# Entry of a two-layer decoder kernel: shift products inside the slab steps of the third pair, and no filler matmuls

## The reference

```python
def modulate(h, shift, scale):
    return h * (1 + scale[:, None, :]) + shift[:, None, :]

mod = c_act @ ada_w[l] + ada_b[l]
sh1, sc1, g1, sh2, sc2, g2, sh3, sc3, g3 = jnp.split(mod, N_MOD, axis=-1)
h = modulate(rms_norm(x, ffn1_norm[l]), sh1, sc1)
x = x + 0.5 * g1[:, None, :] * swiglu(h, ffn1_w_in[l], ffn1_w_out[l])
...
g, u = jnp.split(h @ w_in, 2, axis=-1)
return (jax.nn.silu(g) * u) @ w_out
```

## Time and profile before

| | us |
|---|---|
| runs | 2551.80, 2551.59, 2549.71; median 2551.59 |
| profiled execution, its own time | 2553.98 |
| its span, first to last instruction | 2552.1 |
| PE busy | 2525.7 (99%) |
| DVE busy | 1688.9 (66%) |
| ACT busy | 966.1 (38%) |
| mean granted clock | 0.995 |

### The profile page before, as it was taken

How to read it: one execution, slowest core, us unless ns; L and a number is a source line. 1 busy time by engine, 2 the same in 40 slices (tenths; PEclk the granted TensorE clock), 3 DMA queues, 4 the chain that set the end, 5 groups by cost and what they waited for, 6 DMA issues and landing times.

```text
span 2552.1 us, 34962 instructions
## 1 busy us (share of the span) xinstructions
PE 2525.7 (99%) x11604; PEld 2060.6 (81%) x11604; DVE 1688.9 (66%) x2533; ACT 966.1 (38%) x1628; POOL 108.4 (4%) x187
## 2 busy tenths in 40 slices
PE   8999999999999999999999999999999999999998
PEld 6888888788788878888878888877878888788887
DVE  7655678798988575544365557779999866644432
ACT  3322323555544343332242222255554443423223
POOL 3000010000000000000000001100000000000000
PEclk9899999999999999999999999999999999999999
DMA  8455575322223434543335556722323333333332
GB/s 272 143 157 164 162 230 153 89 80 82 86 85 89 127 88 132 163 132 93 99 89 161 160 164 190 230 79 79 90 82 86 87 95 94 91 97 92 96 97 87
DMA packets 467654, 310.99 MB, mean 122 GB/s; under 512 B 10891, under 2 KB 445181, under 8 KB 467576
## 3 DMA queue, kind: packets, MB, share of 16 engines
q1 hardware_dynamic: 444544, 234.91, 31.5%
q0 software_dynamic: 20352, 70.13, 8.5%
q10 hardware_dynamic: 2696, 5.13, 0.7%
HBM read 305.41 MB, written 5.05 MB: 122 GB/s over the span
## 4 chain that ended last, share of the span: by engine, by line
PE 89%; DVE 5%; ACT 2%; DMA 2%; issue 1%; SPq 0%; ACTq 0%; DVEq 0%
PE bank L1482 27%; PE bank L1484 27%; PE bank L1483 27%; PE bank L1756 2%; DMA w_raw<-in_ffn_w_in 2%; PE bank L1734 1%; DVE rstd L809 1%; DVE w_lo L785 1%; PE bank L1504 1%; DVE scaled L820 1%; PE bank L1726 1%; DVE h_lo L829 1%; PE bank L1505 1%; PE bank L1509 1%; ACT w_hi L435 1%
## 5 line engine op out<-in xcount | busy, mean ns | idle before, releaser
L785 DVE TENSOR_TENSOR w_lo<-w_raw,w_hi 128x1024 fp32r<-128x1024 f32 (+1 forms) x428 | 515.1, 1203 | 539.4 <-ACT w_hi L435 538.8
L1482 PE MATMUL bank<-h_hi,w_hi 128*128 128x512 f32 x2096 | 833.3, 398 | 2.8 <-DVE scaled L1131 2.7
L1484 PE MATMUL bank<-h_hi,w_lo 128*128 128x512 f32 x2096 | 817.5, 390 | 0.0
L1483 PE MATMUL bank<-h_lo,w_hi 128*128 128x512 f32 x2096 | 816.3, 389 | 0.0
L435 ACT ACTIVATE w_hi<-w_raw 128x1024 fp32r<-128x1024 f32 (+1 forms) x428 | 445.3, 1040 | 845.8 <-PE bank L1484 795.1
L1482 PEld LDWEIGHTS bank<-h_hi,w_hi 128*128 128x128 f32 x2096 | 393.6, 188 | 88.2 <-issue 6.4
L1484 PEld LDWEIGHTS bank<-h_hi,w_lo 128*128 128x128 f32 x2096 | 393.4, 188 | 84.4
L1483 PEld LDWEIGHTS bank<-h_lo,w_hi 128*128 128x128 f32 x2096 | 394.1, 188 | 77.5 <-issue 0.5
L1247 DVE SCALAR_TENSOR_TENSOR conv_part<-glu,conv_taps,conv_part 128x512 f32<-128x512 f32 x464 | 320.0, 746 | 0.0
L1482 PE MATMUL bank<-s_hi,w_hi 128*128 128x512 f32 x704 | 275.5, 391 | 0.0
L1484 PE MATMUL bank<-s_hi,w_lo 128*128 128x512 f32 x704 | 274.0, 389 | 0.0
(11 more groups left out here) (262 smaller groups left out, 2711.3 us busy)
## 6 DMA issues: line engine op xcount, KB each, us to landing
w_raw<-in_ffn_w_in SPq DMA_DIRECT2D x176, 512.0 KB, 3.9
ada_raw<-in_ada_w POOLq DMA_DIRECT2D x128, 512.0 KB, 4.9
w_raw<-in_w_mix_in SPq DMA_DIRECT2D x112, 512.0 KB, 3.8
w_raw<-in_ffn_w_out SPq DMA_DIRECT2D x64, 512.0 KB, 3.9
w_raw<-in_ffn_w_out SPq DMA_DIRECT2D x32, 384.0 KB, 3.4
ada_first<-in_ada_w SPq DMA_DIRECT2D x16, 512.0 KB, 8.3
w_raw<-in_w_attn_branch SPq DMA_DIRECT2D x16, 512.0 KB, 3.9
w_raw<-in_w_conv_branch SPq DMA_DIRECT2D x16, 512.0 KB, 3.9
```

The lines of the kernel that those rows point to most:

```text
L785: dve.tensor_tensor(wlo[slot][:, 0:n, :], raw[slot][:, 0:n, :], whi[slot][:, 0:n, :].bitcast(F32), ALU.subtract).then_inc(w_lo[slot], 1)
L1482: pe.matmul(acc, wh, hi[:, k0 + k, :], start=first and k == 0, stop=False)
L1483: pe.matmul(acc, wh, lo[:, k0 + k, :], start=False, stop=False)
L1484: mm = pe.matmul(acc, wl, hi[:, k0 + k, :], start=False, stop=last and k == n - 1)
```

## The change

- `third_pair` takes the place of `two_slabs` for pair 2. Slot 1 runs one step behind slot 0, and each of the 16 slab steps has four of the 64 shift-product matmuls between its three large ones: two behind the first, two behind the second.
- `first_sum(1)` moves from behind pair 1 into it (before k=10); the norm's mean moves from k=5 to k=4.
- DVE reads pair 0's bank 0 (`read_plain(0)`) before it reads the shift half's sum, and bank 1 behind `scaled(1)`. The order in `norm_units` becomes w_lo_third(0), low(0), scaled(1), read_plain(1), scaled(2), low(1), w_lo_third(1).
- x's back halves of blocks 0 and 1 are copied by ACT, those of blocks 2 and 3 by DVE.
- The tap transposes come behind the x transposes, in banks TP, and ACT copies them behind the last `plain_hi`. The tap rows lie elsewhere in SBUF.
- All `keep_busy` calls, the tile of ones and its memset are gone.

```diff
@@ ACT @@
-        act.wait_ge(sem("tapsp_ready"), DEPTH)
-        for l in range(DEPTH):
-            act.activation(CW2[...], G[l][:, 0:HEADS * CK], ACT.Copy).then_inc(sem("cw_ready"), 1)
         act.wait_ge(sem("consts"), 3)
         for t in range(QB):
             act.wait_ge(sem("xp_ready"), 2 * t + 1)
             act.activation(X[:, 0:4, t * P:(t + 1) * P], S[0][:, :]..., ACT.Copy).then_inc(sem("x_front"), 1)
+            if t < 2:
+                act.wait_ge(sem("xp_ready"), 2 * t + 2)
+                act.activation(X[:, 4:KT, t * P:(t + 1) * P], (S[1], AUX)[t][:, :]..., ACT.Copy)\
+                    .then_inc(sem("x_back_act"), 1)
...
             plain_hi(0, j)
+        act.wait_ge(sem("tapsp_ready"), DEPTH)
+        for l in range(DEPTH):
+            act.activation(CW2[...], TP[l][:, 0:HEADS * CK], ACT.Copy).then_inc(sem("cw_ready"), 1)
@@ DVE @@
+        def read_plain(t):
+            dve.wait_ge(sem("plain_done"), t + 1)
+            dve.tensor_tensor((F[1], SQ)[t][:, :], G[t][:, :], RSTD[:, :], ALU.mult).then_inc(acc_read[t], 2)
...
             if first:
                 w_lo_third(0)
                 low(0)
-                read_bank(0)
+                scaled(1)
+                read_plain(1)
                 scaled(2)
+                low(1)
                 w_lo_third(1)
-                low(1)
-                read_bank(1)
                 scaled(3)
                 low(2)
...
-        for t in range(QB):
+        for t in (2, 3):
             x_back(t)
...
         for j in range(2, KT):
+            if j == KT // 2:
+                dve.wait_ge(sem("tapsp_ready"), DEPTH)
             plain_lo(0, j)
...
         first_parts(0, 1)
         norm_begin(0, 0)
+        read_plain(0)
         dve.wait_ge(sem("mod_summed"), 1)
@@ PE @@
+        def third_pair(banks, weights, products):
+            for k in range(KT + 1):
+                for slot, n in ((1, k - 1), (0, k)):
+                    if not 0 <= n < KT:
+                        continue
+                    if n == 0:
+                        pe.wait_ge(w_hi[slot], 3)
+                        pe.wait_ge(w_lo[slot], 3)
+                        pe.wait_ge(acc_read[slot], 2)
+                    if slot == 0:
+                        pe.wait_ge(sem("unit_lo"), n + 1)
+                    wh, wl, acc = weights[0][slot][:, n, :], weights[1][slot][:, n, :], banks[slot][:, :]
+                    pe.matmul(acc, wh, HHI[:, n, :], start=n == 0, stop=False)
+                    for part in range(2):
+                        i = 2 * (2 * k - slot) + part
+                        out, pair_weights = products[i // KT]
+                        shift_product(i // KT % 2, i % KT, out, pair_weights)
+                        if part == 0:
+                            pe.matmul(acc, wh, HLO[:, n, :], start=False, stop=False)
+                    mm = pe.matmul(acc, wl, HHI[:, n, :], start=False, stop=n == KT - 1)
+                    if n == KT - 1:
+                        mm.then_inc(w_used[slot], 1)
...
             plain_slabs(0, G, (whi, wlo))
-            plain_slabs(1, TP, nexts, {5: lambda: norm_mean(0, 0)})
-            keep_busy(6, S[0])
             pe.wait_ge(sem("scale0_ready"), 1)
-            first_sum(1).then_inc(sem("mod_summed"), 1)
-            keep_busy(6, S[0])
+            plain_slabs(1, TP, nexts, {4: lambda: norm_mean(0, 0),
+                                       10: lambda: first_sum(1).then_inc(sem("mod_summed"), 1)})
             pe.wait_ge(sem("shift_parts"), 2)
-            keep_busy(6, S[0])
             pe.wait_ge(sem("aux_read"), 1)
-            two_slabs(2, 2, lambda j: pe.wait_ge(sem("unit_lo"), j + 1), weights=thirds,
-                      at={1: lambda: shift_product(0, S[0], (whi, wlo)), 2: lambda: shift_product(1, S[1], (whi, wlo)),
-                          3: lambda: shift_product(0, O, nexts), 4: lambda: shift_product(1, AUX, nexts)})
+            third_pair(G, thirds, ((S[0], (whi, wlo)), (S[1], (whi, wlo)), (O, nexts), (AUX, nexts)))
...
         for n in range(2 * QB):
             t, half = n // 2, n % 2
-            if n == 4:
+            if n == 6:
                 pe.wait_ge(sem("pt_ready"), 1)
                 pe.wait_ge(sem("selg"), 1)
                 first_sum(0).then_inc(sem("scale0_summed"), 1)
             if t and not half:
-                pe.wait_ge(sem("cw_ready"), DEPTH)
-                keep_busy(2, G[1])
                 pe.wait_ge(sem("x_front"), t)
...
         pe.wait_ge(sem("pt_ready"), 1 + DEPTH)
-        keep_busy(8, G[0])
+        pe.wait_ge(sem("taps_in"), 16 * 2 * DEPTH)
+        for l in range(DEPTH):
+            for h in range(HEADS):
+                mm = pe.transpose(TP[l][...], CWR[0:CK, l, h * P:(h + 1) * P], ident[0:CK, 0:CK])
+            mm.then_inc(sem("tapsp_ready"), 1)
...
-        keep_busy(6, S[0])
         pe.wait_ge(sem("sq_ready"), DEPTH * 3 * KT)
```

More of the change, by code:

```diff
@@ L251, in build @@
     BR = at("bias_row", [P, TOK + P], F32, s0 + 12448)
-    CWR = at("tap_rows", [P, DEPTH, D], F32, h0)
+    CWR = at("tap_rows", [P, DEPTH, D], F32, h0 + 24 * KB)
     YO = at("y_rows", [P, QB, D], F32, h0)
@@ L362, in _ @@
         pool.memset(minus_half[:, :], -0.5).then_inc(sem("minus_half"), 1)
-        pool.memset(busy[:, :].bitcast(F32), 1.0).then_inc(sem("busy_ready"), 1)
         pool.wait_ge(sem("ident0"), 1)
@@ L518, in _ @@
                 .then_inc(sem("x_front"), 1)
+            if t < 2:
+                act.wait_ge(sem("xp_ready"), 2 * t + 2)
+                act.activation(X[:, 4:KT, t * P:(t + 1) * P], (S[1], AUX)[t][:, :].rearrange("p (j t) -> p j t", t=P), ACT.Copy)\
+                    .then_inc(sem("x_back_act"), 1)
         w_hi_part(0, 0)
-        act.wait_ge(sem("cw_ready"), DEPTH)
         act.wait_ge(sem("x_front"), QB)
@@ L525, in _ @@
             if j == 4:
-                act.wait_ge(sem("x_back"), QB)
+                act.wait_ge(sem("x_back_act"), 2)
+                act.wait_ge(sem("x_back"), 2)
             plain_hi(0, j)
+        act.wait_ge(sem("tapsp_ready"), DEPTH)
+        for l in range(DEPTH):
+            act.activation(CW2[:, l * HEADS * CK:(l + 1) * HEADS * CK], TP[l][:, 0:HEADS * CK], ACT.Copy)\
+                .then_inc(sem("cw_ready"), 1)
         for t in range(QB):
@@ L844, in norm_begin @@
                 dve.wait_ge(sem("aux_read"), 1)
-            else:
-                reciprocal(l * AUXN + AUX_NORM[k], l * RSN + RS_NORM[k])
+                norm_scaled(l, k, 0)
+                return
+            reciprocal(l * AUXN + AUX_NORM[k], l * RSN + RS_NORM[k])
             norm_scaled(l, k, 0)
             norm_scaled(l, k, 1)
+        def read_plain(t):
+            dve.wait_ge(sem("plain_done"), t + 1)
+            dve.tensor_tensor((F[1], SQ)[t][:, :], G[t][:, :], RSTD[:, :], ALU.mult).then_inc(acc_read[t], 2)
         def norm_units(l, k, pair, rows):
@@ L860, in read_bank @@
             def read_bank(t):
[L861 to L865, removed]
+                dve.wait_ge(w_used[t], pair + 1)
+                dve.tensor_tensor((F[1], SQ)[t][:, :], G[t][:, :], RSTD[:, :], ALU.mult).then_inc(acc_read[t], 1)
             if first:
@@ L1526, in plain_slabs @@
                         pe.wait_ge(w_lo[slot], pair + 1)
+                        if banks is TP:
+                            pe.wait_ge(sem("cw_ready"), DEPTH)
                     if slot == 0:
@@ L1536, in plain_slabs, with shift_product @@
                         mm.then_inc(sem("plain_read"), 1)
[L1538 to L1543, removed]
+        def shift_product(slot, n, out, weights):
+            pe.matmul(out[:, 0:2], weights[0][slot][:, n, :], SHP[:, 0, n, :], start=n == 0, stop=False)
+            mm = pe.matmul(out[:, 0:2], weights[1][slot][:, n, :], SHP[:, 0, n, :], start=False, stop=n == KT - 1)
+            if n == KT - 1:
[20 more added lines that the diff above has]
+                    mm = pe.matmul(acc, wl, HHI[:, n, :], start=False, stop=n == KT - 1)
+                    if n == KT - 1:
+                        mm.then_inc(w_used[slot], 1)
         def first_entry():
@@ L1595, in norm_mean @@
             mean(aux, SSUM[:, :])
-        def keep_busy(n, out):
-            for _ in range(n):
-                pe.matmul(out[:, :], busy[:, 0:P], busy[:, :], start=True, stop=True)
         def first_sum(n):
@@ L1641, in _ @@
             if t and not half:
-                pe.wait_ge(sem("cw_ready"), DEPTH)
-                keep_busy(2, G[1])
                 pe.wait_ge(sem("x_front"), t)
             if t >= 2 and half:
-                pe.wait_ge(sem("x_back"), t - 1)
+                pe.wait_ge(sem("x_back_act"), t - 1)
             pe.wait_ge(sem(f"x_in{t}"), 16)
@@ L1652, in _ @@
         pe.wait_ge(sem("pt_ready"), 1 + DEPTH)
-        keep_busy(8, G[0])
+        pe.wait_ge(sem("taps_in"), 16 * 2 * DEPTH)
+        for l in range(DEPTH):
+            for h in range(HEADS):
```

(2 more changed lines are left out.)

5 lines of the change are left out of this document (removed).

## The result

The changed kernel takes 2563.09 us (median of five, 2561.85 to 2563.66), the kernel before 2551.50 beside it (2549.13 to 2551.80): 1.0048 times as long, 95% interval 1.0036 to 1.0059, so 11.6 us slower. The forecast was 2564.7, that is +13.1.

What follows compares the result with a forecast made beforehand. The prediction took dense matmuls on PE (89% of the chain) as the bound; +12.8 us at the fourth pair and +0.3 in the tail made +13.1, so 2564.7 us as the median, range 2549.5 to 2567.5.

Steps and rivals of the forecast that it cites:

- (b): Start without fillers: clock at 1.2 GHz when the first dense run starts, +2.4 us, bounds 0 and 2.7.
- (h): Fourth pair: dense work needs 5.4 us to bring the clock back, +2.7 us, bounds 1.5 and 3.4.
- (a): Start: x's copies shared, tap transposes later; first dense run earlier, -1.35 us, bounds 0 and -2.
- (c): Shift half's sum inside the second pair: PE only pays the sum, +0.3 us.
- P: The end of the second pair, predicted at 55.5 us.
- (d): Wait ahead of the third pair: PE idle without filler, starting at P + 1.95 us.
- (e): New wait for the third pair's second weight tile: after step 0, PE waits until P + 5.65 us.
- (f): Third pair's stream: 15 steps stay at 1.2 GHz, 2.13 us each, 32.0 us.
- (g): New wait ahead of the fourth pair, on DVE work queued behind the last shift product: 4.4 us of idle PE.
- (i): Tail without fillers: if the clock falls, the last four transposes take longer, +0.3 us, bounds 0 and 1.
- Rival 1: Third pair's stream brings the clock back at once: no change, 2549 to 2554 us; chance 0.21.
- Rival 2: Clock not lost at the start nor ahead of the stream: 2544.8, up to 2547.5 us; chance 0.07.

Runs made afterwards that it cites:

- fill_waits: The changed kernel with filler matmuls in the two waits ahead of the third pair's stream, 7 and 10: 2546.64 us, 0.9989 of the kernel before.
- both_orders: The changed kernel with the DVE reorderings of early_order and late_order together, no filler: median 2540.62 us, in two groups.
- fill_second: The changed kernel with 10 fillers only in the second wait, between steps 0 and 1 of the third pair: 2548.77 us.
- early_order: The changed kernel with w_lo_third and read_plain(1) earlier on DVE, shortening the two waits ahead of the stream, no filler: median 2558.74 us, in two groups.
- late_order: The changed kernel with DVE's w_lo_part(3,0), pair 1 reads and gate product ahead of w_shift_next, shortening the wait ahead of the fourth pair: 2557.89 us.
- before_no_fill: The kernel before with keep_busy issuing no fillers, nothing else changed: 2551.64 us, 1.0005 of the kernel before.
- before_third: The kernel before with the interleaved third pair alone, its fillers and DVE order kept: 2567.14 us, 1.0066 of the kernel before.
- dense_first: The changed kernel with the 64 shift-product matmuls moved to the third pair's last eight slab steps: 2550.44 us, 1.0000 of the kernel before.

## Why the prediction was right, step by step

The direction, the case and the size held: the forecast case is the one that ran, +11.6 for +13.1. That the sum came within 1.5 us is in part luck, since (b) and (h) turned out to have no fixed size. By its steps, in the profiled execution:

- **(a)** -1.35 was taken. The first dense run's second matmul starts at 31.17; before, its first started at 32.55 and the second 0.33 later, so it is 1.7 earlier. ACT starts w_hi at 24.72 (26.69 before), 2.0 earlier instead of 1.4. The term was 0.35 too small, because of (b)'s surprise: the last x transposes ran at 0.11 us each (23.55 to 24.55, eight and their drain in 1.07), where 0.22 was taken for all.
- **(b)** 2.4 was taken; the profiled execution paid 1.2. The level did stand at 1.2 GHz when the dense run began, and the clock came back at 33.7, when six matmuls had gone from 31.17 to 33.71 in 2.54 us for 1.36 at full clock. The working charged half of 5.4 us of dense work; here 5.7 us passed from 27.98 to the return, but PE ran the first two steps while DVE made the next h_lo, and only what lay behind 31.17 was on the path.
- But (b) has no single value. Up to the end of the second pair the kernels of fill_waits and both_orders give PE the same work as the kernel after, and their traces differ from it. Windows of both_orders, then of fill_waits:

```profile
30.00:36.00 6.00, 5.20 (x13) 4.12 (x13) 5.89 (x9) 6.00 (x12) 0.29 (x1) 0.50 0.98 218
36.00:37.00 1.00, 1.00 (x4) 0.76 (x4) 0.59 (x2) 1.00 (x3) 0.00 (x0) 0.68 1.13 425
...
27.00:40.00 13.00, 11.16 (x47) 8.68 (x48) 12.25 (x16) 11.77 (x22) 5.01 (x7) 1.00 1.04 319
```

- In both_orders the level fell just before 30 and came back at 36.6, and the second pair was over at 55.2; in fill_waits it never fell, and the pair was over at 52.3; in the kernel after it was 53.7. So the same start cost anything from nothing to 2.8 us (in both_orders thirteen matmuls from 30.82 on took 5.71 us for 2.95 at full clock), and the 2.4 that was taken lies inside that. One trace can't size this term.
- The rule of the Trainium skill that was weighed there ("TensorE: Matmul & The Clock Gate", Part 4, PE-mode transpose: transposes do not make the clock engage) doesn't hold here: 24 transposes alone, from 17.94, were followed by eight at half the price. The outcome in this execution was still the one that the rule gave, since the level was lost again in the 2.25 us ahead of 27.98; in the traces of fill_waits and both_orders it was still high there.
- **(c), P.** The sum cost 0.2. The second pair ended at 53.7 (53.46 and the last matmul's 0.23), not 55.5: 1.8 early, of which (b) is 1.2, (a) 0.35 and (c) 0.1. The rest is that the sum started from 54.14 as the pair's end before, where the timeline has PE's next matmul at 53.98.
- **(d), (e)** held: step 0 at P + 1.8 (1.95 was said), step 1 at P + 5.6 (5.65), released by w_lo_third.
- **(f)** held: down at 57.6, steps 2.13 apart, never up in the 32 us of the stream. The reason given, waits around a single step, is what fill_waits bears out, and fill_second for the second of them. It was put more firmly than it deserved: with waits of 0.96 and 0.38 around the step (early_order, both_orders) 5 of 7 and 4 of 12 runs ended in the upper group, by their mean clock with the level lost, and the one wait of 1.63 never cost it.
- **(g)** held: 4.21 of idle PE for 4.4, released by DVE's gate product; late_order took it away and gained 5.2 (4.8 by the ratios).
- **(h)** was 3.0 (11.4 at the matmul of 117.38 less 95.82 - 87.42 = 8.4) for 2.7. The way back isn't of one length: without a wait ahead of it, it was 3.1 us in late_order, 3.8 in before_no_fill (76.38 to 80.2) and 5.4 before; behind the wait, 6.1 here and 4.8 in fill_waits (79.66 to 84.5). So (h) could as well have come out at 2.4.
- **(i)** The last four transposes take 1.09 us for 0.64, 0.45 longer for the 0.4 that was said. From the last slab to the end of the span the traces differ by 0.2 (9.8 less 9.6), where 0.3 was taken.

Rival 1, that the stream would bring the clock back, fell: in 32 us it never did. Rival 2 is real, but of other kernels: fill_waits runs at its level in the stream and at the start. It was given 2544.8 to 2547.5, and fill_waits measured 2546.64.

## What to carry to other kernels

Where dense work sits behind two short waits, look at the granted clock and at what follows them: here streams of large matmuls got the clock back by themselves, within 3.1 to 6.1 us, while the stream with small matmuls between kept the level it started at, so the same microsecond of waiting cost there as much as the stream was long. Before small work is spread between large, ask who on another engine is queued behind its last product: here that was 4.2 us, and one reordering on DVE took it off. And time a kernel that idles near such a place many times, since one run can show either of two values 14 us apart; and don't size a term of the clock's return from one trace.

## What the runs showed of the hardware

- The clock came up during transposes of 128x128 float32 on TensorE alone: about 0.22 us each from 17.94, 0.11 from 23.55 on (kernel after).
- A mix of three 512-column and four 2-column matmuls neither lifted nor lost the level: 32 us at 1.2 GHz in the kernel after, 17 at 2.4 in fill_waits. A 2-column one costs 0.213 us at the low level (2.13 less three at 0.427, over four) and 0.12 at the high one (1.15 less three at 0.227), so its cost nearly doubles with the clock too.
- The same program showed two times at two mean clocks: both_orders 2540.1 to 2540.6 us at 0.997 in eight runs, 2553.8 to 2554.9 at 0.991 to 0.992 in four. One idle stretch of 1.63 us never lost the level in the 11 runs of fill_second. Around one step, waits of 1.08 and 1.57 us (before_third), or 1.63 and 2.42 (kernel after), lost it in every run by their times and mean clocks; the programs traced with 0.96 and 0.38 seem to lose it in some.
- At the low level large matmuls brought it back after 3.1 us (late_order), 3.8 (before_no_fill), 4.5 (dense_first), 4.8 (fill_waits), 5.4 (kernel before) and 6.1 (kernel after).
- With the same work given to PE at the start, the level was never lost (fill_waits, 27 to 40 us), was low from 26.9 to 33.7 (kernel after) or from 29.8 to 36.6 (both_orders).
